# The first weight blocks of a layer kernel in another order, and three row stores moved to ScalarE's queue

## The chip, the cores and the metric

One core of a Trainium2 chip runs the whole program. The metric is the device time of one execution in microseconds (us), as the median of the runs; lower is better.

## What is computed

One transformer layer over 256 tokens of width 2048, all in float32. Nine rows of modulation come from a condition vector, then a gated feed-forward part, a mixer of attention and a recurrence, and a second feed-forward part follow, each normalised, modulated and gated:

```
mod = silu(c) @ w_ada + b_ada                      # 9 rows of 2048: sh1 sc1 gt1 sh2 sc2 gt2 sh3 sc3 gt3
u = rmsnorm(h, norm1_g) * (1 + sc1) + sh1
h = h + 0.5 * gt1 * swiglu(u, ffn1_w_in, ffn1_w_out)
...
h = h + gt2 * mixer(u, ...)
...
h = h + 0.5 * gt3 * swiglu(u, ffn2_w_in, ffn2_w_out)
return rmsnorm(h, final_g)
```

## The kernel before

Everything is a program written out by hand for each engine, with semaphores between them; no scheduler moves anything.

**Products.** A weight chunk of 1 MB (128 partitions x 4 blocks of 512 columns) is loaded by SyncE's queue (SP) into `raw`, a ring of four (`load`, L688, issued at L700). It is used in two *units* of two blocks each. For each unit ScalarE (ACT) casts `raw` to the short float `hi` (`split`, L1452), VectorE (DVE) subtracts for the rest `lo` (`split`, L2040), and TensorE (PE) makes three products into PSUM: `hi` by `act_hi`, `hi` by `act_lo`, `lo` by `act_hi`. That is 12 matmuls of 128x512 in a unit. `unit_used` counts finished units; a `raw` place is loaded again when its old chunk is used up.

**The start.** The columns of `w_ada` that make `sc1` and `sh1` are loaded in 32 tiles of 1 MB, two for each k-tile (128 rows of u). They share SP's queue with the weights (`load_start`, L675, into six homes in `ada_s`, `ada_w` and `gate_w`). DVE reduces each (`start_tile`, L2069), then `start_mod` (L2076 to L2084) scales this k-tile in `n_t`, ACT makes `act_hi` from it (`first_hi`, L1709) and DVE `act_lo` (`start_lo`, L2090). Thus at the start a k-tile becomes ready only every second tile. To have work with few k-tiles, the first 72 units (the table `STAGES`, L51) go over six groups of columns, each with two blocks (the two halves of the gated input). Two groups, a *pair*, fill PSUM's four double banks `pa`, `pb` and `px`, `pq`. An entry of `STAGES` is a pair and the k-tiles that are multiplied for it in that turn; when the pair changes, ACT copies each bank to `part` (`keep`, L1719), and back if that pair was begun before (L1722). The order of ACT's copies between its casts comes from `todo` (L1724 to L1734): a copy stands behind the cast of the unit that is three after the last use of its bank. `tile_unit` (L214) says ahead of which unit DVE reduces a tile, `load_before` (L218) ahead of which chunk SP loads it, `hi_unit` and `lo_unit` (L222, L226) where `act_hi` and `act_lo` of a k-tile stand. PE waits for `act_hi` and `act_lo` of a k-tile at its first unit (L1187, L1195).

**The gate rows.** gt1, gt2 and gt3 are made column-wise in `mod` (one value in each partition and k-tile), but are wanted as a row in all partitions. `store_gate` (L677, issued at L680) writes a row to HBM as 2048 single values of 4 bytes; `load_gate` (L683, issued at L686) waits for that store to have landed and reads the row back into all partitions (`gt_row`). Both stand in SP's program among the weight loads: gt1 is stored in the second input phase of the first feed-forward part (`ffn1_in1`, i = 3, behind its chunk 3) and read back in `ffn1_out1`, gt2 is stored behind the `proj` phase, gt3 in `ffn2_in0` behind chunk 7.

ACT issues four small loads of its own in `ffn1_in2` (`rows_load`, L1778 to L1788): positions (256 values of 4 bytes) and three rows spread over 128 partitions.

Of the kernel before, what the change touches and what calls it, by code (L numbers as in the profile page):

```python
# [33 lines left out]
P = 128  # L34
# [15 lines left out]
GROUPS = 6  # L50
STAGES = [(0, ((0,), (1,))), (1, ((0, 1),)), (2, ((0, 1),)),  # L51
# [30 lines left out]
def build(nc, x, x_t, c, cols, positions, w_ada, w_first, ffn1_w_in, ffn1_w_out, w_proj, w_rest, w_gates,  # L82
# [3 lines left out]
    KD = D // P  # L86
# [56 lines left out]
    SH1, SC1, GT1, SH2, SC2, GT2, SH3, SC3, GT3 = range(9)  # L143
    HALF_ROWS = [(GT1, q) for q in range(4)] + [(m, half) for m in (SH2, SC2, GT2, SH3, SC3, GT3) for half in (0, 1)]
    ROWS_OUT = (GT1, GT2, GT3)
# [50 lines left out]
    def mod_count(m):  # L196

        return [k for k, _ in MODS].index(m) + 1
# [15 lines left out]
    def tile_unit(k):  # L214

        return (0, 0, 1, 2)[k] if k < 4 else 3 + round(2.2 * (k - 4))

    def load_before(k):  # L218

        return k // 2 if k < 4 else tile_unit(k) // 2 + 1  # L220

# [80 lines left out]
    with ExitStack() as ctx:  # L302
# [94 lines left out]
        mod = sb("mod", [P, 9 * KD])  # L397
# [34 lines left out]
        gt1_out = sem("gt1_out")  # L432
# [226 lines left out]
        def _(sp):  # L659
# [16 lines left out]

            def store_gate(m, done):  # L677

                sp.wait_ge(mod_ok, mod_count(m))
                sp.dma_start(gate_rows[ROWS_OUT.index(m):ROWS_OUT.index(m) + 1, :].rearrange("a (k p) -> p (a k)", p=P),  # L680
                             mod[:, m * KD:(m + 1) * KD], allow_slow_non_contiguous=True).then_inc(done, 16)

            def load_gate(row, done, landed):  # L683
# [81 lines left out]
            def load_ffn(f):  # L765
                g0 = 0
                for p, ng in enumerate(PARTS):
                    name = f"ffn{f}_in{p}"
                    def ffn_in(i, first, name=name, g0=g0):
# [12 lines left out]
                        for j in range(8):  # L782
                            if not at_seam(plan[name], i, j):
                                ffn_chunk(name, i, i + g0, j, j)
                            load_ada(plan[name].at(i) + j)
                            if name == "ffn1_in2" and (i, j) in ((1, 4), (1, 7)):
                                load_x_again(2 + (j == 7))
                            if (name, i, j) == ("ffn1_in1", 3, 3):
                                store_gate(GT1, gt1_out)
                            if (name, i, j) == ("ffn2_in0", 0, 4):  # L790
                                load_pair(0, 0)
                                load_pair(0, 1)
                            if (name, i, j) == ("ffn2_in0", 0, 7):
                                store_gate(GT3, gt3_out)
                    over(sp, ng, ffn_in)
# [33 lines left out]
            proj_pair("proj", w_proj)  # L829
            store_gate(GT2, gt2_out)  # L830
            for j in range(4):
# [598 lines left out]
        def _(act):  # L1430
# [273 lines left out]
            def first_body(ph):  # L1704
# [20 lines left out]
                for k, move in enumerate(MOVES):  # L1725
                    todo.setdefault(move[0] + 3, []).append(k)
                assert [k for u in sorted(todo) for k in todo[u]] == list(range(len(MOVES)))
# [29 lines left out]
            def partial_body(ph, i, g, last):  # L1757
# [16 lines left out]
                if last:  # L1774
                    silu(ph)(i)
                    nat_evac_at(nb - 1, i - 1)

            def rows_load(k):  # L1778

# [23 lines left out]
            def first_casts(n_):  # L1803

                if n_ == 10:
                    s_casts("ffn2_in0")
                if n_ >= 12:
                    fast_cast(0, n_ - 12)

            def ffn(f, mid):  # L1810
                for p, ng in enumerate(PARTS):
                    ph = plan[f"ffn{f}_in{p}"]
                    for i in range(ng):
# [4 lines left out]
                        if (f"ffn{f}_in{p}", i) in FAST:  # L1818
                            fast_body(f"ffn{f}_in{p}", i)
                            continue  # L1820
                        in_body(ph, i, i == 0, silu(ph), None, True, mid=mid if p == 0 else None,
                                step=rows_load if (f, p, i) == (1, 2, 0) else
                                first_casts if (f, p, i) == (2, 0, 0) else None)
                        if (f, p, i) == (1, 2, 2):
# [54 lines left out]
            for n_, (j, half, k0, n) in enumerate(units(4, 4)):  # L1879
# [6 lines left out]
                if n_ == 3:  # L1886
                    copy_b(3)

            def qk_silu(hds):
# [1151 lines left out]
```

## Time and profile before

| | |
|---|---|
| median of 3 runs | 2039.84 us (2038.3 to 2039.84) |
| the profiled execution's own time | 2043.58 us |
| its span in the profile | 2041.8 us |
| mean granted TensorE clock | 0.997 of full |
| PE busy | 2019.9 us (99%) |
| DVE busy | 1685.4 us (83%) |
| ACT busy | 1206.6 us (59%) |
| HBM read | 541.28 MB, 266 GB/s over the span |

An engine's busy time is the time that its instructions ran. The granted clock is 1.00 at TensorE's full 2.4 GHz and 0.50 at 1.2 GHz; a slice in between holds both. In the timeline a row is one or several like instructions in a line: start in us from the span's start, us from the first's start to the last's end, engine, line of the kernel, operation, output and inputs, their shapes, how many, and in brackets how long the engine had stood idle before it and who ended that.

### The profile page before, as it was taken

To read this page: it belongs to the slowest core of one execution; us is meant where nothing else is said; L and a number is where in the kernel's file an instruction comes from. 1 tells how busy PE (TensorE), PEld (TensorE's weight loads), DVE (VectorE), ACT (ScalarE), POOL (GpSimd) and SP (SyncE) were. 2 spreads that over 40 slices of the span, in tenths; PEclk is the share of its full clock that TensorE was granted. 3 is DMA by queue.
4 is the path that set the end of the run, shared out by engine and by line. 5 is a ranking of instruction groups with operands and counts; after the bars stand their busy time and mean duration, and the time that the engine had idled before them with its cause. 6 is when DMAs were issued, how large, how long until landed. Compare 5 with 4: busy or idle time off the path is not lost.

```text
span 2041.8 us, 23814 instructions
## 1 busy us (share of the span) xinstructions
PE 2019.9 (99%) x9090; PEld 1662.6 (81%) x9090; DVE 1685.4 (83%) x2208; ACT 1206.6 (59%) x1658; POOL 2.4 (0%) x14
## 2 busy tenths in 40 slices
PE   8999999999999999999999999999999999999998
PEld 6788888887888888888777888888888888888887
DVE  7898698878889988788998898887777777787786
ACT  5777644655345555446555676567775577755764
POOL 0000000000000000000000000000000000000000
PEclk8999999999999999999999999999999999999999
DMA  9998799899999868976665687575565556555554
GB/s 386 393 380 310 286 346 385 329 310 372 364 357 345 311 244 347 343 278 182 221 219 209 237 304 270 184 234 179 206 229 204 192 179 210 209 199 201 173 198 150
DMA packets 102658, 544.96 MB, mean 267 GB/s; under 512 B 17424, under 2 KB 19728, under 8 KB 53776
## 3 DMA queue, kind: packets, MB, share of 16 engines
q1 hardware_dynamic: 101696, 543.30, 73.1%
q8 instruction: 72, 1.18, 0.2%
q14 instruction: 42, 0.34, 0.1%
q10 hardware_dynamic: 848, 0.14, 0.0%
HBM read 541.28 MB, written 2.12 MB: 266 GB/s over the span
## 4 chain that ended last, share of the span: by engine, by line
PE 93%; DMA 3%; DVE 2%; ACT 1%; issue 1%; SPq 0%; DVEq 0%; ACTq 0%
PE pa L934 13%; PE pb L934 13%; PE pa L942 13%; PE pb L942 12%; PE pb L938 12%; PE pa L938 12%; DMA raw<-in_ffn_w_in_dram 2%; PE pa L1028 2%; PE pa L1034 2%; PE pa L1031 2%; DMA raw<-in_w_first_dram 1%; PE pa L949 1%; PE pq L1201 1%; PE pa L1192 1%; PE pb L1201 1%; PE pa L1197 1%
## 5 line engine op out<-in xcount | busy, mean ns | idle before, releaser
L1452 ACT CAST hi<-raw 128x1024 fp32r<-128x1024 f32 (+2 forms) x662 | 679.1, 1034 | 694.9 <-PE pa L942 251.5
L2040 DVE TENSOR_TENSOR lo<-raw,hi 128x1024 fp32r<-128x1024 f32 (+2 forms) x662 | 784.6, 1201 | 277.3 <-ACT hi L1452 274.3
L2057 DVE SCALAR_TENSOR_TENSOR ada_w<-ada_w,cond_row 128x1024 f32<-128x1024 f32 x207 | 247.2, 1218 | 0.0
L934 PE MATMUL pa<-hi,act_hi 128*128 128x512 f32 x800 | 222.0, 393 | 0.0
L934 PE MATMUL pb<-hi,act_hi 128*128 128x512 f32 x800 | 217.1, 393 | 0.1
L942 PE MATMUL pb<-lo,act_hi 128*128 128x512 f32 x800 | 213.9, 389 | 0.0
L942 PE MATMUL pa<-lo,act_hi 128*128 128x512 f32 x784 | 213.6, 389 | 0.0
L938 PE MATMUL pb<-hi,act_lo 128*128 128x512 f32 x784 | 209.8, 389 | 0.0
L938 PE MATMUL pa<-hi,act_lo 128*128 128x512 f32 x720 | 196.0, 389 | 0.0
L942 PEld LDWEIGHTS pb<-lo,act_hi 128*128 128x128 f32 x800 | 150.2, 188 | 31.4
L934 PEld LDWEIGHTS pb<-hi,act_hi 128*128 128x128 f32 x800 | 148.6, 188 | 32.4 <-issue 2.2
L934 PEld LDWEIGHTS pa<-hi,act_hi 128*128 128x128 f32 x800 | 148.6, 188 | 31.8 <-issue 1.7
L938 PEld LDWEIGHTS pb<-hi,act_lo 128*128 128x128 f32 x784 | 147.2, 188 | 30.9
L942 PEld LDWEIGHTS pa<-lo,act_hi 128*128 128x128 f32 x784 | 147.2, 188 | 30.8
L938 PEld LDWEIGHTS pa<-hi,act_lo 128*128 128x128 f32 x720 | 135.2, 188 | 28.6
L1463 ACT COPY hid_t<-buf_a 32x256 f32<-32x256 f32 x240 | 97.0, 404 | 15.2 <-DVE buf_a L2171 11.9
L934 PE MATMUL pa<-hi,hid_hi 128*128 128x512 f32 x376 | 103.8, 391 | 1.6 <-ACT hi L1452 1.6
L942 PE MATMUL pa<-lo,hid_hi 128*128 128x512 f32 x376 | 103.3, 390 | 1.1 <-DVE lo L2040 1.1
L938 PE MATMUL pa<-hi,hid_lo 128*128 128x512 f32 x376 | 103.3, 390 | 0.0
L942 PE MATMUL pb<-lo,hid_hi 128*128 128x512 f32 x372 | 102.5, 388 | 0.0
L934 PE MATMUL pb<-hi,hid_hi 128*128 128x512 f32 x330 | 89.2, 389 | 0.0
L938 PE MATMUL pb<-hi,hid_lo 128*128 128x512 f32 x330 | 89.1, 389 | 0.0
(462 smaller groups left out, 2612.5 us busy)
## 6 DMA issues: line engine op xcount, KB each, us to landing
raw<-in_ffn_w_in_dram SPq DMA_DIRECT2D x107, 1024.0 KB, 5.1
ada_w<-in_w_ada_dram SPq DMA_DIRECT2D x207, 512.0 KB, 6.5
raw<-in_ffn_w_out_dram SPq DMA_DIRECT2D x60, 1024.0 KB, 6.8
raw<-in_w_first_dram SPq DMA_DIRECT2D x48, 1024.0 KB, 6.9
raw<-in_w_gates_dram SPq DMA_DIRECT2D x32, 1024.0 KB, 4.9
raw<-in_w_proj_dram SPq DMA_DIRECT2D x31, 1024.0 KB, 5.7
pair<-in_ffn_w_in_dram SPq DMA_DIRECT2D x20, 1024.0 KB, 6.9
raw<-in_ffn_w_out_dram SPq DMA_DIRECT2D x24, 768.0 KB, 4.6
```

The source lines that it names most:

```text
L934: pe.matmul(bank[:, tt, cols], a_hi[:, k0 + kk, tok], w_hi[:, kk, cols], start=start and kk == 0, stop=False, skip_group_check=on)
L938: pe.matmul(bank[:, tt, cols], a_lo[:, k0 + kk, tok], w_hi[:, kk, cols], start=False, stop=False, skip_group_check=on)
L942: mm = pe.matmul(bank[:, tt, cols], a_hi[:, k0 + kk, tok], w_lo[:, 2 * half + kk, cols], start=False, stop=stop and rest is None and kk == ...
L949: mm = pe.matmul(bank[:, tt, cols], a_lo[:, k0 + kk, tok], w_hi[:, kk, cols], start=False, stop=stop and kk == n - 1, skip_group_check=on)
L1028: pe.matmul(bank, a_hi[:, kk, :], fast_hi(o)[:, kk, :], start=start and kk == 0, stop=False, skip_group_check=True)
L1031: pe.matmul(bank, a_lo[:, kk, :], fast_hi(o)[:, kk, :], start=False, stop=False, skip_group_check=True)
L1034: mm = pe.matmul(bank, a_hi[:, kk, :], fast_lo(o)[:, kk, :], start=False, stop=kk == 1, skip_group_check=True)
L1201: mm = pe.matmul(bank(m)[:, tt, :], act_hi[:, blocks[m][0], tok], w_lo[:, s0 + m, 0:NC], start=False, stop=True, skip_group_check=True)
L1452: act.copy(hi_of(ph, i, j, half)[:, 0:n, 0:w], raw_of(ph, i, j)[:, 2 * half:2 * half + n, 0:w])\
L1463: ins = act.copy(dst, src)
L2040: dve.tensor_tensor(lo_of(ph, i, j)[:, s, 0:w], raw_of(ph, i, j)[:, s, 0:w], hi_of(ph, i, j, half)[:, 0:n, 0:w].bitcast(F32), ALU.subtract)\
L2057: dve.scalar_tensor_tensor(out=wt, in0=wt, scalar=1.0, in1=cond_row[:, half * ADA_W:(half + 1) * ADA_W], op0=ALU.mult, op1=ALU.mult, accum ...
```

## The change

It has three parts.

1. The table. K-tile 0 is now multiplied for the first pair of groups and then for the second (four units), before k-tile 1 for the second pair; k-tile 1 of the first pair is made up for in the sixth entry. The chunks of `w_first` are laid out by the same table, so each is still one load. The number of matmuls is the same.
2. The tiles of `w_ada` behind the second are loaded and reduced later: `tile_unit` and `load_before` change. ACT's copies of the first pair's banks stand one unit behind the last use in place of three.
3. `store_gate` is gone from SP's program and stands in ACT's: gt1 at `ffn1_in1`, i = 3, behind ACT's cast of unit 8; gt3 at `ffn2_in0` behind unit 8; gt2 in the `rest` phase behind unit 5. `load_gate` stays on SP where it was and still waits for the store.

```diff
-STAGES = [(0, ((0,), (1,))), (1, ((0, 1),)), (2, ((0, 1),)),
-          (2, ((2,), (3,))), (1, ((2, 3),)), (0, ((2, 3),)),
+STAGES = [(0, ((0,),)), (1, ((0,), (1,))), (2, ((0, 1),)),
+          (2, ((2,), (3,))), (1, ((2, 3),)), (0, ((1, 2, 3),)),
...
     def tile_unit(k):
-        return (0, 0, 1, 2)[k] if k < 4 else 3 + round(2.2 * (k - 4))
+        return (0, 0, 2, 4)[k] if k < 4 else 5 + round(2.2 * (k - 4))
     def load_before(k):
-        return k // 2 if k < 4 else tile_unit(k) // 2 + 1
+        return (0, 0, 1, 2)[k] if k < 4 else tile_unit(k) // 2 + 1
...
-                            if (name, i, j) == ("ffn1_in1", 3, 3):
-                                store_gate(GT1, gt1_out)
...
-                            if (name, i, j) == ("ffn2_in0", 0, 7):
-                                store_gate(GT3, gt3_out)
...
             proj_pair("proj", w_proj)
-            store_gate(GT2, gt2_out)
...
                 for k, move in enumerate(MOVES):
-                    todo.setdefault(move[0] + 3, []).append(k)
+                    todo.setdefault(move[0] + (1 if move[1] == 0 else 3), []).append(k)
...
+            def store_gate(m, done):
+                act.wait_ge(mod_ok, mod_count(m))
+                act.dma_start(gate_rows[ROWS_OUT.index(m):ROWS_OUT.index(m) + 1, :].rearrange("a (k p) -> p (a k)", p=P),
+                              mod[:, m * KD:(m + 1) * KD], allow_slow_non_contiguous=True).then_inc(done, 16)
+            def first_gate(n_):
+                if n_ == 8:
+                    store_gate(GT1, gt1_out)
...
             def first_casts(n_):
+                if n_ == 8:
+                    store_gate(GT3, gt3_out)
...
                                 step=rows_load if (f, p, i) == (1, 2, 0) else
+                                first_gate if (f, p, i) == (1, 1, 3) else
                                 first_casts if (f, p, i) == (2, 0, 0) else None)
...
                 if n_ == 3:
                     copy_b(3)
+                if n_ == 5:
+                    store_gate(GT2, gt2_out)
```

SP at the program's start, before (`raw` is a weight chunk; `ada_s`, `ada_w` and `gate_w` are homes of `w_ada` tiles; `n_t` is a piece of x, turned):

```order
L700 DMA raw<-in_w_first_dram 128x2048
L675 DMA ada_s<-in_w_ada_dram 128x2048
L675 DMA ada_w<-in_w_ada_dram 128x2048
L700 DMA raw<-in_w_first_dram 128x2048
L742 DMA n_t<-in_x_t_dram 128x512
L675 DMA ada_w<-in_w_ada_dram 128x2048
L700 DMA raw<-in_w_first_dram 128x2048
L675 DMA gate_w<-in_w_ada_dram 128x2048
L700 DMA raw<-in_w_first_dram 128x2048
```

and after the change:

```order
L694 DMA raw<-in_w_first_dram 128x2048
L675 DMA ada_s<-in_w_ada_dram 128x2048
L694 DMA raw<-in_w_first_dram 128x2048
L675 DMA ada_w<-in_w_ada_dram 128x2048
L694 DMA raw<-in_w_first_dram 128x2048
L736 DMA n_t<-in_x_t_dram 128x512
L675 DMA ada_w<-in_w_ada_dram 128x2048
L694 DMA raw<-in_w_first_dram 128x2048
L675 DMA gate_w<-in_w_ada_dram 128x2048
```

The second chunk stands one tile further ahead, the third one tile and the piece of x, the fourth one tile. The fourth tile of `w_ada` (the first `ada_w`, k-tile 1's second) is one chunk later.

ACT at the same place, before, from the first cast on:

```order
L1452 CAST hi<-raw 128x1024
L1709 ACTIVATE act_hi<-n_t,mod 128x256
L1452 CAST hi<-raw 128x1024 x2
L1709 ACTIVATE act_hi<-n_t,mod 128x256
L1452 CAST hi<-raw 128x1024 x3
L1719 COPY part<-pa 128x1024
L1719 COPY part<-pb 128x1024
L1452 CAST hi<-raw 128x1024
L1719 COPY part<-px 128x1024
L1719 COPY part<-pq 128x1024
```

and after:

```order
L1441 CAST hi<-raw 128x1024
L1698 ACTIVATE act_hi<-n_t,mod 128x256
L1441 CAST hi<-raw 128x1024
L1708 COPY part<-pa 128x1024
L1708 COPY part<-pb 128x1024
L1441 CAST hi<-raw 128x1024
L1708 COPY part<-px 128x1024
L1708 COPY part<-pq 128x1024
L1441 CAST hi<-raw 128x1024 x2
L1698 ACTIVATE act_hi<-n_t,mod 128x256
L1441 CAST hi<-raw 128x1024 x3
L1708 COPY part<-pa 128x1024
```

The four copies of the first pair's banks stand behind the second and the third cast in place of the sixth and the seventh. `act_hi` of k-tile 1 stands behind the fifth cast in place of the third.

DVE at the same place, before, from `act_lo` of k-tile 0 on (L2069 reduces a tile):

```order
L2090 SCALAR_TENSOR_TENSOR act_lo<-n_t,mod,act_hi 128x256
L2040 TENSOR_TENSOR lo<-raw,hi 128x1024
L2069 SCALAR_TENSOR_TENSOR ada_s,macc<-ada_s,cond_row 128x2048
L2040 TENSOR_TENSOR lo<-raw,hi 128x1024
L2069 SCALAR_TENSOR_TENSOR ada_w,macc<-ada_w,cond_row 128x2048
```

and after:

```order
L2095 SCALAR_TENSOR_TENSOR act_lo<-n_t,mod,act_hi 128x256
L2045 TENSOR_TENSOR lo<-raw,hi 128x1024 x2
L2074 SCALAR_TENSOR_TENSOR ada_s,macc<-ada_s,cond_row 128x2048
L2045 TENSOR_TENSOR lo<-raw,hi 128x1024 x2
L2074 SCALAR_TENSOR_TENSOR ada_w,macc<-ada_w,cond_row 128x2048
```

Four `lo` stand ahead of the fourth tile, where there were two.

ACT in `ffn1_in1`, i = 3, after the change, from the cast of unit 7 on (`hid_t` are the blocks of the hidden rows that ACT moves):

```order
L1441 CAST hi<-raw 128x1024
L1452 COPY hid_t<-buf_a 32x2x4x32 x2
L1441 CAST hi<-raw 128x1024
L1452 COPY hid_t<-buf_a 32x2x4x32 x2
L1770 DMA gate_rows<-mod 128x16x1
L1441 CAST hi<-raw 128x1024
```

Before, the same rows stand there without the DMA, which SP issued between the loads of the chunks 3 and 4 of this i.

## Rows read from the trace of the kernel before

**Rows 1.** The waits of PE: us in total, times, longest us.

```profile
PE pa L1192 <- ACT act_hi L1709: 3.2, 2, 2.8
...
PE pa L934 <- ACT hi L1452: 1.6, 1, 1.6
PE pa L1028 <- ACT pa L1521: 1.4, 1, 1.4
```

**Rows 2.** The timeline of the start, PE, ACT and DVE.

```profile
19.48 0.70 PE L1192 MATMUL pa<-hi,act_hi 128*128 128x512 f32 x2 [0.38 <-ACT act_hi L1709]
...
24.25 2.28 DVE L2069 SCALAR_TENSOR_TENSOR ada_w<-ada_w,cond_row 128x2048 f32<-128x2048 f32 x1
...
26.81 1.04 ACT L1452 CAST hi<-raw 128x1024 fp32r<-128x1024 f32 x1 [6.53 <-DMA raw<-in_w_first_dram]
26.90 0.48 DVE L2084 SCALAR_TENSOR_TENSOR n_t<-n_t,gain,rs_row 128x256 f32<-128x256 f32 x1
27.76 0.50 ACT L1709 ACTIVATE act_hi<-n_t,mod 128x256 fp32r<-128x256 f32 x1
...
28.41 1.19 PE L1192 MATMUL pa<-hi,act_hi 128*128 128x512 f32 x2 [2.83 <-ACT act_hi L1709]
28.70 1.22 DVE L2040 TENSOR_TENSOR lo<-raw,hi 128x1024 fp32r<-128x1024 f32 x1
...
34.29 1.00 ACT L1719 COPY part<-pa 128x1024 f32<-128x1024 f32 x1
...
36.73 1.07 PE L1192 MATMUL pa<-hi,act_hi 128*128 128x512 f32 x4
...
39.45 1.07 PE L1192 MATMUL pb<-hi,act_hi 128*128 128x512 f32 x4
```

**Rows 3.** Windows of the start: us, busy by engine, PEclk, DMA share, GB/s.

```profile
13.00:14.00 1.00, 1.00 (x11) 1.00 (x10) 1.00 (x1) 0.00 (x0) 0.00 (x0) 0.92 0.97 410
...
17.00:18.00 1.00, 0.98 (x8) 0.75 (x6) 0.96 (x3) 0.13 (x1) 0.00 (x0) 0.87 1.01 426
...
27.00:28.00 1.00, 0.00 (x0) 0.00 (x0) 0.39 (x1) 1.00 (x2) 0.00 (x0) 0.75 0.99 418
...
34.00:35.00 1.00, 1.00 (x5) 0.79 (x4) 0.87 (x2) 1.00 (x2) 0.00 (x0) 0.84 1.03 434
```

**Rows 4.** SP's timeline around the store of gt1 and its reading back.

```profile
424.99 0.53 SPq L680 DMA_DIRECT2D gate_rows<-mod  x1
...
471.54 0.43 SPq L686 DMA_DIRECT2D gt_row<-gate_rows  x1
```

**Rows 5.** ACT's timeline behind the store of gt1.

```profile
444.83 1.05 ACT L1452 CAST hi<-raw 128x1024 fp32r<-128x1024 f32 x1 [7.93 <-DMA raw<-in_ffn_w_in_dram]
```

**Rows 6.** Windows ahead of, in and behind the store of gt1.

```profile
400.00:410.00 10.00, 10.00 (x46) 8.29 (x45) 7.37 (x10) 7.89 (x11) 0.00 (x0) 1.00 1.01 384
...
433.00:435.00 2.00, 2.00 (x10) 1.68 (x9) 1.93 (x7) 1.21 (x3) 0.00 (x0) 1.00 0.36 16
...
480.00:490.00 10.00, 7.32 (x32) 5.43 (x31) 6.91 (x9) 8.40 (x15) 0.00 (x0) 1.00 0.63 239
```

**Rows 7.** The timeline of SP and ACT around the store of gt3.

```profile
1353.95 0.43 SPq L680 DMA_DIRECT2D gate_rows<-mod  x1
...
1373.16 2.00 ACT L1452 CAST hi<-raw 128x1024 fp32r<-128x1024 f32 x2 [5.38 <-DMA raw<-in_ffn_w_in_dram]
```

**Rows 8.** DMA issues by line: count, KB each, median us to landing.

```profile
gate_rows<-mod SPq DMA_DIRECT2D x3, 8.0 KB, 15.9
...
gb_row<-in_b_fgate_dram ACTq DMA_DIRECT2D x1, 2.0 KB, 8.8
```

**Rows 9.** ACT's own small loads: the first and the last of four.

```profile
554.79 0.39 ACTq L1781 DMA_DIRECT2D pos_i<-in_positions_dram  x1
...
560.20 0.42 ACTq L1788 DMA_DIRECT2D gb_row<-in_b_fgate_dram  x1
```

**Rows 10.** A window in which they are under way.

```profile
555.00:560.00 5.00, 5.00 (x24) 4.14 (x23) 4.14 (x5) 2.01 (x3) 0.00 (x0) 1.00 1.03 425
```

More of the change, by code:

```diff
@@ L675, in load_start @@
                 sp.dma_start(start_home(k), w_ada[m * KD + kt, :, :]).then_inc(ada_s_in[k % S_RING], 16)
[L677 to L681, printed above, removed]
             def load_gate(row, done, landed):
```

## The prediction

> **What bounds the kernel now.** TensorE. I read the table of busy times first (PE 99% of the span), then PE's waits, because only time in which PE stands, or runs at half clock, can be won by an edit that leaves the number of matmuls alone. Behind the start PE waits at two places only: for `hi` in the second output phase, and for a copy of `pa` at the first fast product of the second feed-forward part [rows 1]. In between it runs without a gap, as the stretch from 400 to 410 us shows, with 10.00 us of PE in 10.00 [rows 6]. So I looked at three places.
>
> *The start* [rows 2]. PE begins on units at 19.48. K-tile 1 is wanted by the third unit, and PE stands 2.83 us ahead of it, until 28.41. The bracket names `act_hi`, but ACT's cast of the second chunk (26.81) stands ahead of that `act_hi` in its program and had itself waited 6.53 us for the load: the DMA ends this wait. A unit at full clock takes 2.72 us (36.73 to 39.45), yet the two units from 28.41 took until 36.73, 8.32 us: the clock fell to half during the gap and was full again only in the slice from 34 to 35 [rows 3]. The fifth unit starts at 36.73; that is the mark for everything below.
>
> *gt1* [rows 4 to 6]. SP issues the store at 424.99. The next chunk's cast waits 7.93 us for its load and starts at 444.83; in the middle of this the DMA engines move 16 GB/s, where they had moved 384. PE itself still has work, but ACT and DVE have to make up for the delay, and PE loses 10.00 - 7.32 = 2.68 us between 480 and 490.
>
> *gt3* [rows 7]. The store is issued at 1353.95, ACT's cast at 1373.16 has waited 5.38 us for a load, and PE waits 1.4 us for the copy of `pa` behind it [rows 1]. Of all the waits behind the start, each one follows a store; the store of gt2 is followed by none.
>
> **The start after the change, step by step.** All durations are those of rows 2.
> - Before, three loads of 1 MB lay between the landing of the first chunk and of the second, now two. At 418 GB/s [rows 3] 1 MB (1.05 million bytes) is 2.5 us, so the second chunk lands at 26.8 - 2.5 = 24.3.
> - Units 1 and 2 (k-tile 0, first pair) now have no tile between their two `lo`, so PE runs through: 19.48 + 2 x 2.72 = 24.9. The third unit is k-tile 0 of the second pair. It needs its `hi` (24.3 + 1.04 = 25.4) and the banks `pa`, `pb`, which ACT copies from 22.2 on (2 x 1.00, done at 24.2, in time). PE stands 0.5, starts at 25.4 and ends at 28.1.
> - ACT then copies `px` and `pq` (25.4 to 27.4) and casts unit 4, done at 28.4. PE stands 0.3 and ends unit 4 at 31.2. Here the copies stand ahead of a cast that PE waits for: this wait is new.
> - The fifth unit is k-tile 1. DVE's program has the fourth tile behind the `lo` of unit 4: 28.4 + 1.22 = 29.7. From a tile's start to the end of `n_t` it takes 3.13 us (24.25 to 26.90 + 0.48), then ACT's `act_hi` 0.50: 33.3. So PE stands 2.1 us, and starts the fifth unit at 33.3 instead of 36.73: **3.4 us ahead**.
> - Behind it DVE is late: `act_lo`, `lo`, the fifth tile and `lo` again (about 0.5 + 1.2 + 2.3 + 1.2) end at 38.5. PE wants the last 8 matmuls into unit 6, at 33.3 + 2.72 + 1.81 = 37.8: 0.7 lost. At full clock **2.7 us** are left.
> - The clock. It fell twice, from about 13.9 to 17.3 and from about 27.5 to 34.3 [rows 3]; when it fell the second time PE had stood since 25.6 (28.41 - 2.83). The new gap of 2.1 is not much shorter, so I expect a fall, of the shorter kind: 3.4 us at half speed cost 1.7, but then DVE's 0.7 is covered. Left: 3.4 - 1.7 = **1.7 us**. The bounds are 2.7 (no fall) and 3.4 - 2.95 = 0.45 (as long as before, 28.41 to 34.3).
>
> Later tiles are two units later than before, but PE reaches their k-tiles at the same units or later; with 2.3 us of tile in every 2.2 units of 2.72 DVE keeps up. The copies of the later switches stand as they did. I cost this at nothing; the cover is DVE's slack of two to three units, and if it is short the third k-tile pair stalls by one `n_t` chain, under 1 us.
>
> **The stores.** What an issue costs ACT is an instruction of some 0.4 us on its queue [rows 9], beside its casts; PE is two units behind ACT there, so nothing. None waits for `mod`: the gate rows are made long before. What changes is the transfer. No row of before shows this store on ACT's queue. From below: it lands as fast as on SP's queue, 15.9 us [rows 8]. From above: ACT's four own loads are 256 + 3 x 128 = 640 small pieces and took from 554.79 to 560.20 + 8.8 = 569.0, 14.2 us, beside full traffic [rows 8, 9]; 2048 pieces at this pace are 45 us. I lean to the upper half, since the traffic is as dense around gt1. What it takes from the weights is between nothing (425 GB/s were moved while the first of the small loads were under way, as much as ever [rows 10]) and all of what it takes now, some 10 us of the engines. I take the row nearest to it, the small loads: the weights pass between the pieces, each chunk lands about as usual, and the waits that followed the stores go. gt3: 1.4; no `w_ada` tiles are loaded there any more, and a chunk of 1.05 million bytes in every two units (5.44 us) is 193 GB/s, under half of what the engines move. gt1: up to 2.7; I take 2.0, because SP reaches the reading back of gt1 near 470 [rows 4], while the store, issued by ACT near 439 (the cast's wait began at 444.83 - 7.93 = 436.9, then one cast and two copies), lands between 455 and 484; some of the delay may come back there. gt2: nothing, before and after.
>
> The Trainium skill, "DMA: Bandwidth & Descriptors", section "Issuing engines are not separate DMA queues", says that transfers started from different engines run on the same 16 DMA engines and interleave, and that starting them from several engines saves only issue time. By that rule the stores would give nothing, and the sum would be 1.7 instead of 5.1. The windows agree in one thing, that the DMA engines are shared; what interleaving does to a chunk behind the store no row here shows.
>
> **Sum:** 1.7 + 2.0 + 1.4 = 5.1 us. Against the profiled execution's own 2043.6 that is 2038.5. The median of the runs is 3.7 lower, so **2034.7 us**. Own range of this case: 2033.0 (2.7 + 2.7 + 1.4 = 6.8) to 2036.5.
>
> **Rivals.**
> 1. *The stores' waits stay; only the start gains.* For: the engines are shared, and at 384 GB/s of about 425 there is little room ahead of gt1 [rows 6]. Against: rows 10, and the weights no longer stand behind 2048 pieces in one queue. 2039.8 - 1.7 = 2038.1.
> 2. *The stores gain, the start doesn't.* The clock stays low as long as before. For: the gap of 2.1 us and two shorter ones ahead of it. 2039.8 - 0.45 - 3.4 = 2036.0. If neither gains: 2039.4.
> 3. *Slower: SP is held at the reading back of gt1.* `load_gate` waits for the store, and all weight loads are queued behind it. At 45 us the store lands at 484, SP stands from 470 to 484, and the chunk due at about 473 is issued 11 us late. It decides from about 7 us of lateness: three chunks in the ring are 16.3 us of PE, less 5 for the transfer (2.5 for the chunk, 2.5 for a tile and the row that share the queue) and 4 for cast and `lo` of a unit with their turn on ACT and DVE. PE loses 11 - 7 = 4, and the 2.7 of before stay with it. That gives 2039.8 - 1.7 - 1.4 + 4 = 2040.7. The store's pieces are writes, those of the loads reads; with a pace slower by a tenth it is 4.5 more, 2045.2, and slower than a run can tell from no change.
> 4. *The change doesn't do what it says:* the programs of all engines show it in place; no chance of weight.
>
> **Chances.** Forecast 0.50; rival 1 0.20; rival 2 0.15 (0.06 more where neither gains); rival 3 0.09. About 0.2% (4.1 us) is what a measurement can tell from no change: faster means under 2035.8, slower over 2043.9. Faster: most of the forecast and a part of rival 2, 0.50. Slower: the bad half of rival 3, 0.05. Within 0.2%: 0.45. The range, 2032.5 to 2039.6, takes in the forecast, rivals 1 and 2 and the case without gain.
>
> **What would show it.** In the new profile: the second chunk's cast near 24.3 and the fifth unit near 33.3; two gaps of 0.3 to 0.5 and one near 2.1 ahead of it; granted clock at half for some 3 us behind it. No PE wait between 450 and 500 and at the first fast product; a landing time of the gate stores between 16 and 45 us, and no window at 16 GB/s. Wrong would be: a gap ahead of the fifth unit near 3 or none; the cast behind the gt1 store again 7 us late; or SP's reading back of gt1 followed by a late chunk and a wait of PE.

## The result, and the profile after

The change made the kernel slower. The changed kernel takes 2048.15 us (median of 4 executions, 2047.72 to 2050.59) where the kernel before takes 2039.84: a ratio of 1.0044, 95% interval 1.0028 to 1.0060 (5.7 to 12.2 us). The medians differ by 8.3 us, and the ratio alone gives 9.0. Forecast were 2034.7 us, with 2032.5 to 2039.6 as the range, and a chance of 0.05 for slower.

The profiled execution of the changed kernel took 2048.32 us (span 2046.6), as much as its median. That of the kernel before took 3.7 us more than its median. So the two profiles differ by only 4.7 us, and the missing 3.6 have to be found too; experiment 4 does that.

TensorE's waits in the changed kernel, with their count and the longest (compare [rows 1]):

```profile
engine line waited for: us in total, times, longest us
PE pq L1363 <- DVE m_st L2809: 4.9, 1, 4.9
PE pa L923 <- ACT hi L1441: 4.1, 2, 2.6
...
PE pa L1181 <- ACT act_hi L1698: 2.3, 2, 1.9
```

The 3.2 of `act_hi` have become 2.3, and the wait for a copy of `pa` at the first fast product is gone. But the wait for `hi` has grown from 1.6 to 4.1 (2.56 near 483 and 1.53 near 953; the kernel before also waited 1.1 for `lo` near 489), and a wait of 4.9 has come that the kernel before did not have, in the heads of the attention, on `m_st`. I take the places in order.

**The start.** PE's timeline: start and length in us, engine, line, operation; in brackets how long PE stood before it.

```profile
start us, us, engine line op out<-in xcount [idle before <-releaser]
25.22 0.73 PE L1181 MATMUL pa<-hi,act_hi 128*128 128x512 f32 x2 [0.24 <-ACT hi L1441]
...
28.10 0.63 PE L1181 MATMUL px<-hi,act_hi 128*128 128x512 f32 x2
...
32.94 0.70 PE L1181 MATMUL pa<-hi,act_hi 128*128 128x512 f32 x2 [1.92 <-ACT act_hi L1698]
...
37.85 0.73 PE L1190 MATMUL px<-lo,act_hi 128*128 128x512 f32 x2
38.88 1.08 PE L1181 MATMUL pa<-hi,act_hi 128*128 128x512 f32 x4
```

Third unit at 25.2 (forecast 25.4), fifth at 32.9 (33.3) behind a gap of 1.9 (2.1), a short `lo` wait ahead of 37.85. The 0.3 forecast ahead of the fourth unit (28.10) did not come. The seventh unit starts at 38.88. In the first profile of before that mark is at 36.73 + 2 x 2.72 = 42.17 [rows 2], so this start is 3.3 us ahead of that profile. It ran at full clock throughout, as not every execution does (experiment 4).

**gt1.** The stretches in which the store is under way and in which PE pays for it; the columns are busy time of PE, PEld, DVE, ACT and POOL with instruction counts, granted clock, DMA share and GB/s:

```profile
core 0: us, PE busy (x) PEld busy (x) DVE busy (x) ACT busy (x) POOL busy (x), PEclk, DMA share, GB/s
435.00:440.00 5.00, 5.00 (x24) 4.14 (x23) 3.56 (x5) 2.26 (x4) 0.00 (x0) 1.00 1.31 257
440.00:445.00 5.00, 5.00 (x23) 4.14 (x23) 3.55 (x5) 4.34 (x7) 0.00 (x0) 1.00 1.00 75
...
480.00:490.00 10.00, 7.44 (x26) 5.92 (x26) 8.87 (x12) 5.32 (x7) 0.00 (x0) 0.83 0.67 249
```

The hole in the traffic is still there, at 75 GB/s. The store is issued 8.6 us later than before (433.59 against 424.99) and takes longer to land, 28.2 us against 16.0. It lands at 461.8, ahead of the reading back at 468.31. PE still loses 2.56 us between 480 and 490 (2.68 before [rows 6]), and now the clock falls behind it: 0.83 over 10 us is 3.4 us at half speed, 1.7 us of work. The store's issue is gone from SP, and nothing was won.

**gt3.** Here the wait went, as forecast: PE is busy in 50.00 of the 50 us from 1350 on, where it waited 1.4 before [rows 1].

**gt2.** This is where the time went. The row of ACT's own queue, then SP's four loads of `gates` chunks and the tile behind them, ACT's cast, DVE's tile and its `m_st`, PE's two waits and the unit behind them, from the timelines of these engines:

```profile
935.28 0.41 ACTq L1770 DMA_DIRECT2D gate_rows<-mod  x1
...
935.27 9.70 SPq L694 DMA_DIRECT2D raw<-in_w_gates_dram  x4
945.01 0.75 SPq L668 DMA_DIRECT2D gate_w<-in_w_ada_dram  x1
...
952.34 2.00 ACT L1441 CAST hi<-raw 128x1024 fp32r<-128x1024 f32 x2 [4.33 <-DMA raw<-in_w_gates_dram]
...
958.53 1.23 DVE L2062 SCALAR_TENSOR_TENSOR gate_w<-gate_w,cond_row 128x1024 f32<-128x1024 f32 x1 [2.76 <-DMA gate_w<-in_w_ada_dram]
...
964.88 0.16 DVE L2809 TENSOR_SCALAR m_st<-m_st 128x4 f32<-128x4 f32 x1
...
953.43 1.21 PE L923 MATMUL pa<-hi,act_hi 128*128 128x512 f32 x4 [1.53 <-ACT hi L1441]
965.19 0.87 PE L1363 MATMUL pq<-ident,w_sb 128*128 128x128 f32 x3 [4.90 <-DVE m_st L2809]
965.71 2.06 PE L923 MATMUL pa<-hi,act_hi 128*128 128x512 f32 x4
...
970.88 1.08 PE L923 MATMUL pa<-hi,act_hi 128*128 128x512 f32 x4
```

and the same stretch by windows:

```profile
940.00:945.00 5.00, 5.00 (x41) 4.91 (x41) 4.05 (x8) 4.46 (x11) 0.00 (x0) 1.00 1.26 56
945.00:950.00 5.00, 5.00 (x26) 4.17 (x25) 2.71 (x8) 3.00 (x6) 0.00 (x0) 1.00 0.87 103
950.00:955.00 5.00, 3.47 (x16) 2.51 (x15) 1.59 (x2) 2.17 (x3) 0.00 (x0) 1.00 0.96 352
955.00:960.00 5.00, 5.00 (x27) 3.58 (x25) 2.24 (x4) 4.97 (x8) 0.00 (x0) 1.00 1.01 423
960.00:965.00 5.00, 0.29 (x2) 0.00 (x0) 4.90 (x14) 0.25 (x1) 0.00 (x0) 0.89 0.65 220
965.00:970.00 5.00, 4.81 (x13) 3.97 (x14) 3.60 (x11) 3.26 (x11) 0.00 (x0) 0.50 0.02 3
```

Read them as a chain. The store and the first of the four loads that refill the ring for `gates` are issued in the same microsecond. From 940 to 950 the DMA engines are busy but move 56 and 103 GB/s. ACT's cast waits 4.33 us for its chunk, DVE another 2.76 for its tile, and DVE's program has the row maxima `m_st` of the heads behind this tile; from 958.53 on DVE works without a gap until they are done near 965. PE stands 1.53 and then 4.90 us, 6.43 in all, and when it starts again the clock is at half. In the kernel before, PE was busy in 29.94 of the 30 us from 940 on. The work at half speed costs another 2.3 us: the 12 matmuls from 965.71 took 5.17 us to the start of the next unit, where the same 12 take 2.87 in `change_turned` (experiment 3), which has the same program here and full clock. So this place costs 8.7 us.

### The profile page after: what moved, and what is told of

Its sections match the earlier page's. It is cut to its first block, busy times and chain, and to the rows that moved or that the text cites. A ratio compares the mean times of both kernels' runs of the same rounds, so it can differ in the third digit from the quotient of the medians.

```text
span 2046.6 us, 23810 instructions
## 1 busy us (share of the span) xinstructions
PE 2019.8 (99%) x9090; PEld 1663.5 (81%) x9090; DVE 1686.1 (82%) x2208; ACT 1206.4 (59%) x1658; POOL 2.4 (0%) x14
## 4 chain that ended last, share of the span: by engine, by line
PE 93%; DMA 2%; DVE 2%; ACT 1%; issue 0%; SPq 0%; DVEq 0%; ACTq 0%
PE pa L923 13%; PE pa L931 13%; PE pb L923 12%; PE pb L931 12%; PE pb L927 12%; PE pa L927 12%; PE pa L1023 2%; PE pa L1017 2%; PE pa L1020 2%; PE pa L938 1%; DVE lo L2045 1%; DMA raw<-in_ffn_w_in_dram 1%; PE pb L1190 1%; PE px L1190 1%; PE pq L1190 1%; PE px L1186 1%
```

## The experiments

Theory A says: a gate store takes the DMA engines away from the weights for about 10 us, whichever queue it is issued on, and the moment decides what that costs; the start gains. Its rivals are that ACT's queue itself is the trouble, and that the new start costs something later. Ratios are to the kernel before, with 95% intervals. Its own median was 2038.86 to 2039.72 us in the sets of runs below, so kernels of different sets are compared by their ratios.

### 1. The parts of the change, each alone

`start_only` has the table, `tile_unit`, `load_before` and the copies of the change, and the stores on SP as before; `stores_only` is the other half.

`start_only`, as the change but for:

```diff
@@ SP's program @@
+            def store_gate(m, done):
...
+                            if (name, i, j) == ("ffn1_in1", 3, 3):
+                                store_gate(GT1, gt1_out)
...
+                            if (name, i, j) == ("ffn2_in0", 0, 7):
+                                store_gate(GT3, gt3_out)
...
             proj_pair("proj", w_proj)
+            store_gate(GT2, gt2_out)
@@ ACT's program @@
-            def store_gate(m, done):
...
-                if n_ == 5:
-                    store_gate(GT2, gt2_out)
```

`stores_only`, as the change but for the old values of `tile_unit` and `load_before` and:

```diff
-STAGES = [(0, ((0,),)), (1, ((0,), (1,))), (2, ((0, 1),)),
-          (2, ((2,), (3,))), (1, ((2, 3),)), (0, ((1, 2, 3),)),
+STAGES = [(0, ((0,), (1,))), (1, ((0, 1),)), (2, ((0, 1),)),
+          (2, ((2,), (3,))), (1, ((2, 3),)), (0, ((2, 3),)),
...
-                    todo.setdefault(move[0] + (1 if move[1] == 0 else 3), []).append(k)
+                    todo.setdefault(move[0] + 3, []).append(k)
```

> The change's table, tiles and copies, with all three gate stores where they were before (SP's queue, old places). Theory A (the start gains what its rows show, and the loss is all in the stores): units run about 3 us earlier from the fifth on, nothing else moves, so about 2039.8 - 3.5 = 2036.3, between 2035 and 2037.5, and PE's waits behind 440 us are those of before. Rival B (the new start itself costs something later, for instance by tiles of w_ada that come two units later): 2040 or more, with a wait of PE somewhere behind 100 us that the kernel before did not have.

> The start of the kernel before, with the three gate stores on ACT's queue at the places of the change. Theory A: the loss of the change (8.3) plus what its start gained (3.5): about 2051.6, between 2049 and 2053, with PE's long wait near 960 us. Rival B: the stores alone cost less than the whole, 2042 to 2047. If the loss at gt2 needs the 3 us of lead that the start gives (a coincidence of times), 2038 to 2041.

Measured: `start_only` 2037.17 us, 0.9993 (0.9984 to 1.0002), or 1.4 less than before. The direction of theory A, but less than half of its 3.5, and the interval takes in no gain at all. `stores_only` 2048.81 us, 1.0050 (1.0036 to 1.0064), or 10.2 more. The loss is all in the stores, and it doesn't need the lead of the new start.

### 2. gt2's store: which queue, and when

Four kernels move gt2's store alone, with the rest of the change in place.

`gt2_on_sp` has it on SP's queue behind the loads of `proj`, where it was before:

```diff
             proj_pair("proj", w_proj)
+            store_gate(GT2, gt2_out)
...
-                if n_ == 5:
-                    store_gate(GT2, gt2_out)
```

`gt2_sp_late` has it on SP's queue behind the first chunk of `gates`, `gt2_act_early` on ACT's in the last step of `proj`, `gt2_act_later` on ACT's in the second step of `gates`; the call at n_ == 5 goes in these too:

```diff
@@ gt2_sp_late @@
                             load(plan[name], i, j, src, 4)
+                        if (name, i, j) == ("gates", 0, 0):
+                            store_gate(GT2, gt2_out)
@@ gt2_act_early @@
+                if n_ == 11:
+                    store_gate(GT2, gt2_out)
@@ gt2_act_later @@
+                if (i, n_) == (1, 5):
+                    store_gate(GT2, gt2_out)
```

> The changed kernel with gt2's store alone put back on SP's queue behind the loads of proj; gt1's and gt3's stay on ACT's. Theory A (gt2's store at its new place costs 6.4 us of PE standing and some 2.3 us of half clock): 2048.2 - 8.7 = 2039.5, between 2037 and 2041, no PE wait between 900 and 1000 us. Rival C (the loss is spread over all three stores, since their pieces go between those of the weights): 2043 to 2046.

> The changed kernel with gt2's store still on ACT's queue, but behind the copy of the last proj bank (near 913 us in place of 935), about where SP issued it before. Theory A1 (the moment decides, not the queue): as with gt2 on SP, 2037 to 2041, no PE wait between 900 and 1000. Rival A2 (ACT's queue decides: there the small writes go between the pieces of the weights, and hold up every chunk): 2045 to 2049, with the waits at the gates phase or in front of it.

> The changed kernel with gt2's store on SP's queue, but late: behind the load of the first chunk of gates, near 935 us, the moment at which the change issues it from ACT. Theory A1 (the moment decides): the chunks of gates behind it in the queue land late all the same, PE waits some 5 to 8 us between 945 and 970, and the time is 2045 to 2050. Rival A2 (ACT's queue decides): 2037 to 2041, no such wait.

> The changed kernel with gt2's store on ACT's queue in the steady part of the gates phase, in its second step at unit 5, near 1005 us, where chunks and tiles ask for 220 GB/s and the ring is full. Theory A1: the ring's lead covers it, 2037 to 2041. Rival A2 (ACT's queue, wherever it is full of weights): 2043 or more, with a wait of PE within 30 us behind the store. If the gates phase itself, with its chain through DVE, bears no late chunk at all, it is also 2043 or more, so this case speaks for A1 only if it comes out fast.

Measured:

| kernel | queue | issued | us | ratio (95%) |
|---|---|---|---|---|
| the change | ACT | 935 | 2048.15 | 1.0044 (1.0028 to 1.0060) |
| gt2_sp_late | SP | 937 | 2048.75 | 1.0042 (1.0027 to 1.0057) |
| gt2_on_sp | SP | 912 | 2038.01 | 0.9997 (0.9988 to 1.0006) |
| gt2_act_early | ACT | 911 | 2038.82 | 0.9999 (0.9990 to 1.0007) |
| gt2_act_later | ACT | 1005 | 2041.15 | 1.0013 (1.0004 to 1.0022) |

The pairs at one moment (935 and 937, 911 and 912) cost the same on either queue, and on one queue two moments differ by 9 us. For gt2's store the queue is without effect; the moment makes it. The windows of `gt2_sp_late` have the same hole as those of the change:

```profile
940.00:945.00 5.00, 5.00 (x43) 5.00 (x43) 4.81 (x12) 4.97 (x10) 0.00 (x0) 1.00 0.69 72
945.00:950.00 5.00, 5.00 (x28) 4.28 (x28) 2.15 (x6) 3.73 (x8) 0.00 (x0) 1.00 0.80 41
```

and `gt2_act_early` has it too, only where nobody waits for a chunk:

```profile
915.00:920.00 5.00, 5.00 (x25) 4.15 (x24) 4.41 (x8) 2.48 (x3) 0.00 (x0) 1.00 0.21 15
920.00:925.00 5.00, 5.00 (x23) 4.13 (x22) 4.37 (x11) 1.54 (x2) 0.00 (x0) 1.00 0.80 59
```

The kernel before has that hole as well; I had not read its windows there, since no wait of PE followed. They are:

```profile
920.00:925.00 5.00, 5.00 (x25) 4.15 (x24) 4.41 (x8) 2.48 (x3) 0.00 (x0) 1.00 0.48 19
925.00:930.00 5.00, 5.00 (x24) 4.13 (x23) 4.41 (x9) 1.53 (x2) 0.00 (x0) 1.00 0.75 85
```

`gt2_act_later` missed both expectations. In steady traffic the store leaves a hole of 48 GB/s, and PE pays less, though not nothing: it waits 1.25 and 2.04 us, both times for DVE, which is late with the heads. Its window, and PE's two waits:

```profile
1010.00:1015.00 5.00, 5.00 (x25) 4.11 (x24) 0.41 (x4) 4.08 (x12) 0.00 (x0) 1.00 1.16 48
...
1028.21 0.65 PE L1333 MATMUL px<-p_t,proj 128*64 128x256 f32 x4 [1.25 <-DVE p_t L2833]
1034.09 1.17 PE L1312 MATMUL pq<-k_t,q_t 64*128 64x128 f32 x6 [2.04 <-DVE proj L2891]
```

### 3. What in the store makes the hole

If the hole grew with the number of elements, four stores of 512 elements would each make a small one, which the ring covers.

`quarters` is `start_only` with these stores, gt1's at four places of `ffn1_in1` and gt3's at four of `ffn2_in0`; the reading back waits for all four.

```diff
+                row = ROWS_OUT.index(m)
-                sp.dma_start(gate_rows[ROWS_OUT.index(m):ROWS_OUT.index(m) + 1, :].rearrange("a (k p) -> p (a k)", p=P),
-                             mod[:, m * KD:(m + 1) * KD], allow_slow_non_contiguous=True).then_inc(done, 16)
+                sp.dma_start(gate_rows[row:row + 1, q * P:(q + n) * P].rearrange("a (k p) -> p (a k)", p=P),
+                             mod[:, m * KD + q:m * KD + q + n], allow_slow_non_contiguous=True).then_inc(done, 16)
```

> The start of the change, gt2's store on SP's queue where it was, and gt1's and gt3's stores on SP's queue in four pieces each, 512 elements apiece, gt1's at 371, 392, 414 and 436 us, gt3's two chunks apart. If a store costs the engines in proportion to its elements, each piece delays the next chunk by 2 to 3 us, which the ring covers: PE's wait near 485 (1.6 to 2.7 us) and that at the first fast product (0.7 to 1.4) go, and the time is that of the start alone less 2: about 2035. If a store's cost is fixed and not by elements, four pieces are worse than one: 2040 or more.

Measured: 2043.72 us, 1.0020 (1.0011 to 1.0029). Worse than one whole store each: PE now waits 0.6 us at 433, 1.5 at 456, 2.6 at 486 and 1.5 at 1367. The DMA issues of this kernel give the pieces' landing times (KB each, median us to landing),

```profile
gate_rows<-mod SPq DMA_DIRECT2D x8, 2.0 KB, 12.1
gate_rows<-mod SPq DMA_DIRECT2D x1, 8.0 KB, 14.2
```

and its windows the deepest of the holes behind gt1's pieces:

```profile
375.00:380.00 5.00, 5.00 (x24) 4.13 (x22) 5.00 (x7) 2.25 (x3) 0.00 (x0) 1.00 0.50 34
```

A quarter of the elements takes 12.1 us to land against 14.2 for a whole store. Not every hole is as deep as this one: in windows of 2.5 us the traffic behind gt1's four pieces falls to 33, 100, 136 and 69 GB/s. But together they cost more than the whole stores (1.0020 against 0.9993). So cutting the store in time raised its cost here. It left two theories: P, that it is the tiny pieces (4 bytes each, since every partition holds 16 elements that go to 16 places 512 bytes apart); Q, that any write among the loads costs this. To tell them apart VectorE first turns the 16 columns in blocks of 32 by 32, so that 32 neighbours of the row lie in one partition:

```diff
+                if m in ROWS_OUT:
+                    dve.wait_ge(pad_ok, 1)
+                    link(dve.tensor_tensor(gate_pad[:, 0:KD], mod[:, cols_], bada[:, cols_], ALU.add))
+                    dve.transpose(gate_tr[:, ROWS_OUT.index(m), :], gate_pad[:, :]).then_inc(mod_ok, 1)
+                    return
...
-                act.dma_start(gate_rows[ROWS_OUT.index(m):ROWS_OUT.index(m) + 1, :].rearrange("a (k p) -> p (a k)", p=P),
-                              mod[:, m * KD:(m + 1) * KD], allow_slow_non_contiguous=True).then_inc(done, 16)
+                row = ROWS_OUT.index(m)
+                for b in range(4):
+                    act.dma_start(gate_rows[row:row + 1, :].rearrange("a (k b r) -> (a k) b r", k=KD, b=4)[:, b, :],
+                                  gate_tr[32 * b:32 * b + KD, row, :]).then_inc(done, 16)
```

`change_turned` is the whole change with this, at its moments and on ACT's queue; `turned` is `start_only` with it; `before_turned` is the kernel before with it. `gt1_early` asks in another way whether the wait near 485 comes from gt1's store: `start_only` with this store, whole, at i = 2, j = 0 instead of i = 3, j = 3.

> The whole change, stores on ACT's queue at its places, but VectorE first turns the gate's 16 columns in blocks of 32 by 32, and each gate is stored in four transfers of 16 pieces of 128 bytes: 64 pieces in place of 2048. Theory P (it is the count of tiny pieces that stops the weights): no window under 100 GB/s behind the stores, no wait of PE near 485, 953 and 960 us, no fall of the clock there, and the time is below that of the new start alone: 2034 to 2037 (median of before taken as 2039.5). Rival Q (any write to the chip's memory among the loads costs some 10 us of the engines, whatever its pieces): 2045 to 2049, as the change. The quarter stores, each nearly as disturbing as a whole, speak for Q; that they cost so much could also be their queueing behind loads.

> The new start with the turned stores on SP's queue at the places of the kernel before. Theory P: 2034 to 2037, and no wait of PE behind the stores of gt1 and gt3. Rival Q: as the start alone, 2037 to 2039, with the waits near 485 and at the first fast product as they were. If the wait near 485 stays but the windows behind the store are full, that wait belongs to the reading back of the row and not to the store.

> The new start, all stores whole on SP's queue; gt1's store 60 us earlier (near 365 us, where SP has its first chunk of the third step), the others where they were. If the loss near 485 comes from this store alone, it goes away, and unless the stall comes up again behind 365, the time is that of the start alone less 1.5: 2034.5 to 2037. If the stall only moves, PE waits somewhere between 380 and 400 instead, and the time is 2037 to 2040. If the wait near 485 stays with the store long landed, the reading back of the row near 470 makes it.

> The kernel before with nothing changed but the three stores, turned and in 64 pieces of 128 bytes each, on SP's queue at their old places. With the new start the turned stores gave a ratio of 0.9975. If the start is worth the 1.4 to 1.7 us that the profiles show at the seventh unit, this one is at 0.9982 to 0.9984, near 2036; if most of the gain lay in the stores and the start gives nothing once they are harmless, it is 0.9975 as well, near 2034.5; no PE wait near 485 or at the first fast product in either case.

Measured:

| kernel | us | ratio (95%) |
|---|---|---|
| change_turned | 2034.31 | 0.9976 (0.9966 to 0.9986) |
| turned | 2034.15 | 0.9975 (0.9965 to 0.9984) |
| gt1_early | 2035.99 | 0.9980 (0.9972 to 0.9989) |
| before_turned | 2036.62 | 0.9987 (0.9978 to 0.9996) |

Theory P, against Q. With nothing but the form of the stores changed, the changed kernel goes from 1.0044 to 0.9976, and beats the kernel before. Two more things follow from the table. The stores cost 0.0013 of the time (2.7 us) at their old places, by `before_turned`, and 0.0068 (13.9 us) at the places of the change. And once they are turned, `turned` and `change_turned` are equal: moving the stores to ACT's queue gains nothing even when they are harmless. The DMA issues of `change_turned` have the row

```profile
gate_rows<-gate_tr ACTq DMA_DIRECT2D x12, 2.0 KB, 4.6
```

and these are the windows behind gt1's and gt2's stores, the places that had 75, 56 and 103 GB/s:

```profile
435.00:440.00 5.00, 5.00 (x23) 4.13 (x22) 3.15 (x5) 3.72 (x6) 0.00 (x0) 1.00 0.93 372
440.00:445.00 5.00, 5.00 (x24) 4.13 (x23) 4.21 (x7) 3.68 (x6) 0.00 (x0) 1.00 1.08 361
...
935.00:940.00 5.00, 5.00 (x43) 5.00 (x43) 4.41 (x12) 4.97 (x9) 0.00 (x0) 1.00 0.97 326
940.00:945.00 5.00, 5.00 (x29) 4.30 (x29) 2.66 (x6) 5.00 (x11) 0.00 (x0) 1.00 0.94 362
945.00:950.00 5.00, 5.00 (x25) 4.20 (x24) 4.90 (x12) 4.97 (x9) 0.00 (x0) 1.00 0.44 156
```

The fall to 156 in the last row is no hole: the ring is full, the DMA engines idle more than half the time, and PE waits for nothing. PE's waits in this kernel are those of the start alone:

```profile
PE pq L1164 <- DVE st L2622: 3.4, 1, 3.4
PE pa L1155 <- ACT cond L1846: 3.1, 1, 3.1
PE pa L1185 <- ACT act_hi L1702: 2.3, 2, 1.9
```

What the turning costs is in the timeline of DVE in `turned`, 0.21 us three times:

```profile
320.82 0.21 DVE L2057 STREAM_TRANSPOSE gate_tr<-gate_pad 128x32 f32<-128x32 f32 x1
```

`gt1_early` says that the wait near 485 is the store's and not that of the reading back, which stayed where it was: with the store at 364 PE is busy in 20.00 of the 20 us from 480 on, and none of PE's waits in this kernel lies between 364 and 480. There the ring bears the same hole. The windows:

```profile
369.00:374.00 5.00, 5.00 (x28) 4.22 (x27) 2.67 (x6) 2.59 (x4) 0.00 (x0) 1.00 0.65 33
...
480.00:500.00 20.00, 20.00 (x89) 16.34 (x88) 19.09 (x26) 7.71 (x9) 0.00 (x0) 1.00 0.90 340
```

The gain against `start_only` is 0.0013, or 2.6 us, with an error as large. PE stood 1.55 there in that profile.

`turned` against `before_turned` gives the start once more: 0.9987 - 0.9975 is 0.0012, or 2.4 us, against 1.4 from `start_only`; the error of the first is 2.7 and of the second 1.8. Neither of the two expectations of `before_turned` is hit (0.9982 to 0.9984, or 0.9975), with 0.9987; it lies on the side of the first, a start that keeps its worth when the stores are harmless, but the 0.0012 between the two kernels is within its error.

### 4. The kernel before, profiled again

> The kernel before once more, for a second profile. In its first profile the clock was at half from 27.5 to 34.3 us, and that execution took 3.7 us more than the median. The kernel with the old start and the moved stores shows no such fall in its profile. If the fall is a matter of the single execution, this one shows none, and a time near 2039; if it belongs to the old start, it shows it again, and a time near 2043.

This is one execution: 2039.15 us, a span of 2037.4, 4.4 us under that of its first profile. PE's timeline at the start, and then the windows with the clock, both of this second profile:

```profile
28.40 1.19 PE L1192 MATMUL pa<-hi,act_hi 128*128 128x512 f32 x2 [2.65 <-ACT act_hi L1709]
...
35.42 1.16 PE L1192 MATMUL pa<-hi,act_hi 128*128 128x512 f32 x4
...
40.98 1.07 PE L1192 MATMUL px<-hi,act_hi 128*128 128x512 f32 x4
```

```profile
27.00:28.00 1.00, 0.00 (x0) 0.00 (x0) 0.52 (x2) 1.00 (x2) 0.00 (x0) 0.91 1.01 426
28.00:29.00 1.00, 0.60 (x2) 0.54 (x3) 0.71 (x2) 1.00 (x2) 0.00 (x0) 0.50 0.99 418
...
31.00:32.00 1.00, 1.00 (x5) 0.77 (x5) 1.00 (x1) 0.00 (x0) 0.00 (x0) 0.89 0.99 418
```

The clock was at half for 3.4 us, not for 6.8 as in the first profile [rows 3]. The fifth unit starts at 35.42 where it started at 36.73, the seventh at 40.98. In `stores_only`, with the same start, it did not fall at all there. So the fall is a matter of the single execution. The other profiles say the same, and of the new start too. Counted from the start of the first unit, the seventh starts after:

| start | clock behind the gap | us | profiles |
|---|---|---|---|
| old | at half for 6.8 us | 22.7 | the first of before |
| old | at half for 3.4 us | 21.2, 21.3 | before_turned, before_again |
| old | full | 21.0 | stores_only |
| new | at half for 3.4 us | 20.8 | gt2_on_sp, gt2_sp_late, gt2_act_later, quarters, gt1_early, change_turned |
| new | full | 19.6 | the change, start_only, gt2_act_early, turned |

The gap ahead of the fifth unit is 1.9 us in all ten profiles of the new start, with a fall and without. Like against like, the new start is ahead by 1.4 us without a fall and by 0.4 to 0.5 with one of 3.4 us. The first profile of before also held longer waits, 2.68 us near 485 and 1.4 at the first fast product, where the second has 1.45 and 0.4. So 1.2 us at the seventh unit (42.17 against 40.98) and 2.2 of waits make 3.4 of the 4.4 between the two spans: the profile on which I forecast was of an execution with more to gain than most.

## Why the prediction was wrong

**The start: -1.7 forecast, -1.4 and -2.4 measured, with errors of 1.8 and 2.7.** The size isn't contradicted, and no more than that. Most steps hold: 25.4, 33.3 and 37.8 were 25.2, 32.9 and 37.9. The clock step was right for the new start in six profiles of ten: a fall of 3.4 us, and the seventh unit 20.8 us behind the first, where the forecast's numbers give 42.17 - 1.7 - 19.48 = 21.0. In the other four there was no fall (19.6). It was wrong for the old start: I took the fall of 6.8 us in the one profile of before as a property of it, and three other profiles of that start had 3.4, 3.4 and 0. So a gain near the forecast one comes only where the old start falls and the new one doesn't (1.6 to 1.7), or where the old falls for as long as in that profile. That the comparisons of runs come out near 1.7 is in part luck.

**The step that failed is "gt2: nothing, before and after".** I had priced its issue on ACT (0.4 us, hidden) and read from the missing wait that its transfer is harmless. It was not harmless before, only covered: the traffic was at 19 GB/s for 5 us, in the stretch between the last chunks of `proj` and the narrow ones of `rest`, where nobody was short. The change moves this store past SP's loads of `rest` to the refill of the ring for `gates`, and there the same hole costs 6.4 us of standing PE and 2.3 of half clock. Measured, with gt2's store put back: 0.0047 of the time, or 9.6 us. None of my rivals had it; the one on the slower side looked at SP held by the reading back of gt1, and SP was not held: the store had landed at 461.8, the reading back was issued at 468.31 and the next chunk at 469.05.

**gt1: up to -2.7 forecast, 2.0 taken; nothing gained.** The step that failed is "the weights pass between the pieces". The row I took for it, the loads of small pieces beside 425 GB/s [rows 9, 10], was of reads, 640 pieces in four transfers; this is a write of 2048. They are not alike: the traffic falls to 75 GB/s. Whether it is the writing or the count that sets them apart, no run shows. The wait is 2.56, with 1.7 of half clock behind it. That is no accident of one execution: all six profiles with this store on ACT's queue have a wait of 2.2 to 2.6 there and a clock of 0.83 from 480 to 490 behind it, and the store lands after 22.3 to 32.6 us. The three with it on SP's queue at its old place wait 1.45, 1.55 and 2.68 in two pieces, with full clock, and it lands after 13.9 to 16.0. So the move made gt1 worse, by 1.2 to 2.8 us in the profiles. Queue and moment (433 to 436 in place of 421 to 425) changed together here, and no run parts them. `gt2_on_sp` against `start_only` (gt1 and gt3 moved, gt2 not) gives both stores together: 0.0004 or 0.8 us slower, with an error of 2.6, which takes in the loss at gt1 less the gain at gt3.

**gt3: -1.4 forecast.** The wait went in the changed kernel, as forecast. But it was 1.4 only in the first profile of before; the other three with this store whole on SP's queue had 0.4, 0.7 and 0.3. The term is -0.3 to -0.7.

**Rival 1** was the right reading of the stores: the Trainium skill, "DMA: Bandwidth & Descriptors", section "Issuing engines are not separate DMA queues", says that starting transfers from several engines saves issue time alone. The runs of gt2's store agree: at the same moment it costs 1.0042 on SP's queue and 1.0044 on ACT's. I drew from it only that the gains could fail to come. What it also means is that the moved store takes its hole along, to wherever the new engine happens to issue it.

**The sum.** -1.4 to -2.4 for the start, -0.3 to -0.7 for gt3, +8.7 to +9.6 for gt2, and +1.2 to +2.8 for gt1. That is 6.8 to 10.7 us against a measured 8.3 (5.7 to 12.2).

## What to carry to other kernels

Look for what a transfer does to the traffic (a window with few GB/s while loads are under way; the DMA share of such windows was 0.21 to 1.26 here, so it doesn't mark them), and not only for a wait behind it: a hole that nobody feels is a debt that falls due when the transfer is moved. Moving gt2's store to another queue changed its cost by its moment alone, so ask what loads are issued within 10 us of the new place. Here it was better to mend the pieces: one turn of 0.21 us on VectorE for each store, with 128 bytes a piece in place of 4, made all three stores harmless at the places of the change.

## What the runs showed of the hardware that I had not expected

- A store of 2048 pieces of 4 bytes, 8 KB in all, holds the traffic of the weights at 15 to 75 GB/s in the deepest window of 5 us shown behind it, on either queue. Otherwise 350 to 425 GB/s are moved around gt1, and some 200 in the thinner traffic ahead of gt2's old place. One of 512 such pieces takes nearly as long to land (12.1 us against 14.2). The same 8 KB in 64 pieces of 128 bytes leaves 361 to 372 GB/s in the windows of 5 us behind it, and its four parts land in 4.6 us (median). The Trainium skill, "DMA: Bandwidth & Descriptors", section "Specifications", gives 512 bytes as the least transfer for full rate. No run here stored in pieces of that size; 64 pieces of 128 bytes were enough to leave the weights their rate. Whether the number of pieces or their size does this isn't settled: the turning changed both, and the partitions that they are read from too, and no run had few pieces of 4 bytes or many of 128.
- TensorE's clock fell to half behind gaps of 1.9 to 2.8 us at the start in some executions and not in others of the same start: for 6.8, 3.4, 3.4 and 0 us in four profiles of the old one, for 3.4 in six and 0 in four of the new. A single profile can't price such a fall.
- Later in the kernel a wait in one piece of 2.2 to 2.6 us near 483 was followed by 3.4 us at half clock in all seven profiles that had it (the six above and `quarters`), and two waits of 1.57 and 1.11 us near the same place by none. Where PE has work, 3.4 us at half clock are 1.7 us of work lost. Behind the gap of 4.90 us at 965 the clock stood at half in the whole window from 965 to 970, and the unit there took 2.3 us more.
